# A third fixed expert in the second block of a two-layer mixture-of-experts transformer kernel

## The reference

```python
g_idx = jnp.argmax(g_logits, axis=-1)             # 1 of 4 groups a token
top_v, top_i = lax.top_k(e_sel, MOE_TOP_K)        # 2 of its 8 experts
eid = (g_idx[:, None] * MOE_EXPERTS_PER_GROUP + top_i).reshape(-1)
...
def expert_block(args):
    xb, e = args
    return (jax.nn.silu(xb @ w_gate[e]) * (xb @ w_up[e])) @ w_down[e]
```

## Time and profile before

| | |
|---|---|
| median of three runs | 1744.14 us |
| the profiled execution | 1743.2 us |
| its span | 1741.4 us |
| mean granted TensorE clock | 0.973 of full speed |
| TensorE busy | 1624.5 us (93%) |
| VectorE busy | 653.8 us (38%) |
| ScalarE busy | 373.2 us (21%) |

### The profile page before, as it was taken

One profiled execution on the slowest core, in us unless ns is written; L12 is line 12 of the kernel. 1 busy time (PEld: TensorE's weight loads), 2 busy tenths in 40 slices (PEclk: granted clock), 3 DMA queues, 4 the chain that ended last, 5 costly groups with the idle time before them and its releaser, 6 DMA issues.

```text
span 1741.4 us, 17712 instructions
## 1 busy us (share of the span) xinstructions
PE 1624.5 (93%) x6682; PEld 700.8 (40%) x6682; DVE 653.8 (38%) x1382; ACT 373.2 (21%) x919; POOL 71.2 (4%) x91
## 2 busy tenths in 40 slices
PE   5989998988999997998899999998889999979996
PEld 2435454462343332332344455444453333323332
DVE  2676665351323322323476122224531322322331
ACT  3023444231001010010410334333320101001000
POOL 1100000100000000000000000001000000000000
PEclk9999999999999998999999999998999999989999
DMA  9983823179999999999977021033389999999997
GB/s 353 372 308 100 288 97 146 52 285 389 430 426 426 425 428 427 427 428 419 364 240 243 1 97 49 1 124 123 141 365 420 427 423 427 429 426 426 428 427 293
DMA packets 109478, 526.64 MB, mean 302 GB/s; under 512 B 7921, under 2 KB 49122, under 8 KB 84682
## 3 DMA queue, kind: packets, MB, share of 16 engines
q1 hardware_dynamic: 80080, 486.56, 68.7%
q10 hardware_dynamic: 21322, 19.63, 3.6%
q0 software_dynamic: 7984, 19.22, 3.0%
HBM read 524.44 MB, written 8.48 MB: 306 GB/s over the span
## 4 chain that ended last, share of the span: by engine, by line
PE 81%; DMA 9%; DVE 5%; issue 2%; ACT 1%; SPq 1%; ACTq 0%; DVEq 0%
PE psum L2259 20%; PE psum L2290 11%; PE psum L2305 10%; PE psum L2016 10%; PE psum L1816 7%; PE psum L1988 4%; PE psum L1871 3%; DMA XN<-in_moe_w_up_dram 3%; DMA ring<-in_moe_w_up_dram 3%; DMA HT<-in_moe_w_down_dram 2%; PE psum L2237 2%; DVE W L1154 2%; DMA ring<-in_ada_w_dram 1%; PE psum L2123 1%; PE psum L1999 1%
## 5 line engine op out<-in xcount | busy, mean ns | idle before, releaser
L2259 PE MATMUL psum<-ring,V 128*32 128x512 f32 (+2 forms) x1376 | 352.3, 617 | 17.3 <-issue 9.4
L2305 PE MATMUL psum<-V,W 128*128 128x512 f32 x448 | 218.6, 613 | 3.6 <-DVE X L1606 1.1
L1606 DVE TENSOR_TENSOR X<-X,psum 128x512 f32<-128x512 f32 x224 | 153.7, 687 | 109.4 <-PE psum L2305 109.0
L2259 PEld LDWEIGHTS psum<-ring,V 128*32 128x32 f32 (+2 forms) x1376 | 115.9, 134 | 192.9 <-issue 192.6
L2290 PE MATMUL psum<-ring,V 128*64 128x512 f32 (+2 forms) x608 | 181.0, 596 | 0.8 <-issue 0.8
L1154 DVE SCALAR_TENSOR_TENSOR W<-ring,cact,W 128x512 f32<-128x512 f32 (+1 forms) x224 | 138.4, 618 | 7.7
L1046 ACT ACTIVATE V<-psum,modall,scls 128x128 f32<-128x128 f32 x216 | 81.2, 456 | 272.5 <-PE psum L2237 255.6
L2305 PEld LDWEIGHTS psum<-V,W 128*128 128x128 f32 x448 | 72.4, 188 | 148.5 <-DVE X L1606 85.3
L1055 ACT ACTIVATE V<-psum 128x512 f32<-128x512 f32 x28 | 16.7, 597 | 510.3 <-PE psum L2268 399.2
L2259 PE MATMUL psum<-HT,V 128*64 128x512 f32 (+2 forms) x224 | 102.4, 611 | 17.9 <-DMA XN<-in_moe_w_up_dram 17.5
L1816 PE MATMUL psum<-HT,ring 128*128 128x512 f32 x256 | 116.8, 602 | 0.0
(11 more groups left out here) (334 smaller groups left out, 1836.6 us busy)
## 6 DMA issues: line engine op xcount, KB each, us to landing
ring<-in_moe_w_up_dram SPq DMA_DIRECT2D x45, 2048.0 KB, 25.6
ring<-in_moe_w_gate_dram SPq DMA_DIRECT2D x41, 2048.0 KB, 25.3
ring<-in_moe_w_down_dram SPq DMA_DIRECT2D x38, 2048.0 KB, 25.4
ring<-in_ada_w_dram SPq DMA_DIRECT2D x16, 2048.0 KB, 15.8
HT<-in_moe_w_gate_dram SPq DMA_DIRECT2D x10, 2048.0 KB, 23.8
XN<-in_moe_w_up_dram SPq DMA_DIRECT2D x8, 2048.0 KB, 23.8
ring<-in_ada_w_dram ACTq DMA_DIRECT2D x16, 1024.0 KB, 5.2
T<-in_moe_w_up_dram SPq DMA_DIRECT2D x7, 2048.0 KB, 27.4
```

Source lines behind the costliest of these rows:

```text
L1606: return dve.tensor_tensor(x3[:, c, cols], x3[:, c, cols], sum_bank(p, hf, c), ALU.add)
L2259: ins = pe.matmul(bank[2 + 2 * i + b][half * w:(half + 1) * w, :], V[:, col:col + w], slot3(x)[:, k, :], start=(k == 0), stop=(k == KC - 1))
L2305: pe.matmul(sum_bank(p, hf, c), PICK[p % 2][:, c * P:(c + 1) * P], Y[:, hf * HALF:(hf + 1) * HALF], start=True, stop=True).then_inc(s["sum ...
```

## The change

Three things change. Expert 2 becomes the third fixed expert (`FIXED = 3`). The first four entries of `COLS` become 0, 5, 10, 1, so block 1 is now a pair and the four comes second; the pair holds expert 2 in its first half and the expert ranked highest below the wide ones in its other half (`rank_of`). Its matrices are loaded as gate, up, gate, up: loads 6 and 7 are expert 2's and need no ids, loads 8 and 9 are the ranked expert's. Block 2, the four, has loads 10 to 17, and block 1's downs are loads 18 and 19. The homes are dealt out anew (`HOMES`): in layer 0 T comes one place earlier, before ring buffer 4; in layer 1 T comes before ring buffer 5. And loads 9 and 10, the first into freed homes, are made in two halves: the first 1 MB of each when the gate pass of block 0 is half done (`first_gates`, a new semaphore), the second when that pass has ended. VectorE gets the arithmetic that puts expert 2 into its half block.

```diff
-HOMES = ((0, 1, 2, 4, 8, 7, 5, 3, 6), (1, 2, 3, 4, 0, 7, 5, 8, 6))
+HOMES = ((0, 1, 2, 8, 4, 7, 5, 3, 6), (1, 2, 3, 4, 0, 7, 8, 5, 6))
-FIXED = 2
+FIXED = 3
-COLS = [0, 10, 1, 5, 2, 11, 3, 6, 7, 12, 4, 8, 9, 13]
+COLS = [0, 5, 10, 1, 2, 11, 3, 6, 7, 12, 4, 8, 9, 13]
...
+    if COLS[p] == WIDE + 1 and half == 0:
+        return FIXED - 1
-    first = {1: FIXED + COLS[p] - 1, 2: FIXED + WIDE + 2 * (COLS[p] - WIDE - 1), 4: NARROW + 4 * (COLS[p] - WIDE - PAIRS)}
+    first = {1: FIXED + COLS[p] - 1, 2: FIXED + WIDE - 1 + 2 * (COLS[p] - WIDE - 1), 4: NARROW + 4 * (COLS[p] - WIDE - PAIRS)}
...
-    order = gate_up(0) + [(0, "d", half) for half in range(halves(0))] + gate_up(1)
+    order = gate_up(0) + [(0, "d", half) for half in range(halves(0))]
+    order += [(1, kind, half) for half in range(halves(1)) for kind in "gu"]
...
+REFILL = (len(HOMES[0]), len(HOMES[0]) + 1)
...
+                    if i in REFILL:
+                        sp.wait_ge(first_gates, l + 1)
+                        src = {"g": g, "u": u}[kind]
+                        sp.dma_start(slot(m + i)[:, 0:2 * D], src[:, 0:2 * D]).then_inc(w_in[SLOT[m + i]], 16)
+                        refill[i] = src
+                        if i == REFILL[1]:
+                            for x in REFILL:
+                                slot_free(m + x)
+                                sp.dma_start(slot(m + x)[:, 2 * D:4 * D], refill[x][:, 2 * D:4 * D]).then_inc(w_in[SLOT[m + x]], 16)
+                        continue
...
-                dve.tensor_tensor(extra, extra, wide_more, ALU.add)
+                dve.tensor_scalar(third, rank, -1.0, float(4 * WIDE), ALU.is_equal, ALU.mult)
+                step(dve.tensor_tensor(wide_more, wide_more, fixed_less, ALU.add))
                 step(dve.scalar_tensor_tensor(base, wide_base, 2.0, base, ALU.mult, ALU.add))
-                step(dve.tensor_tensor(extra, extra, fixed_less, ALU.add))
+                step(dve.scalar_tensor_tensor(base, wide_more, -1.0 / QP, base, ALU.mult, ALU.add))
+                step(dve.tensor_tensor(extra, extra, wide_more, ALU.add))
+                step(dve.tensor_tensor(base, base, third, ALU.add))
...
+                            if p == 0 and i == 0 and k == 3:
+                                ins.then_inc(first_gates, 1)
```

More of the change, by code:

```diff
@@ L156 @@
 AT = {b: n for n, b in enumerate(ORDER)}
-DMAS = [2 if kind == "kq" else 1 for kind, _, _ in ORDER]
+REFILL = (len(HOMES[0]), len(HOMES[0]) + 1)
+DMAS = [2 if kind == "kq" or kind == "moe" and i in REFILL else 1 for kind, _, i in ORDER]
 ARRIVED = [16 * sum(DMAS[i] for i in range(n + 1) if SLOT[i] == SLOT[n]) for n in range(len(ORDER))]
@@ L448, in program @@
         d_rest, odd_scale = [sem("d_rest0"), sem("d_rest1")], sem("odd_scale")
+        first_gates = sem("first_gates")
         half_sq, odd_ready = sem("half_sq"), sem("odd_ready")
@@ L530, in _ @@
                 m = AT["moe", l, 0]
-                expert, ranked = {}, False
+                expert, ranked, refill = {}, False, {}
                 for i, (p, kind, half) in enumerate(MOE_ORDER):
@@ L1414, in _ @@
                 wide_more, wide_base = (W[:, 784 + 32 * i:816 + 32 * i] for i in (3, 4))
+                third = W[:, 816:816 + E]
                 first_at, fixed_less = W[:, 3776:3784], W[:, 3784:3816]
@@ L1494, in _ @@
                 dve.tensor_copy(eid[:, :], bank[0][:, 0:E]).then_inc(s["eid_ready"].sem, 1)
-                step(dve.scalar_tensor_tensor(first_at.rearrange("p (c e) -> p c e", c=TC), M3[:, :, 0:FIXED], float(-P),
-                                              ranks[:, :, 0:FIXED], ALU.mult, ALU.add))
+                step(dve.scalar_tensor_tensor(first_at.rearrange("p (c e) -> p c e", c=TC), M3[:, :, 0:2], float(-P),
+                                              ranks[:, :, 0:2], ALU.mult, ALU.add))
                 dve.tensor_tensor(FIRST.rearrange("p (a n) -> p a n", n=2 * QP),
```

## The result

The changed kernel takes 1750.91 us (median of 16 runs, 1746.96 to 1753.8) against 1744.37 us for the kernel before (16 runs, 1743.36 to 1748.19). The ratio is 1.0033, with a 95% interval of 1.0026 to 1.0040: slower by about 6 us. I had forecast 1745.0 with a range of 1739.0 to 1750.0, and held a change too small to tell (under about 0.2%) for the likeliest case.

The account below looks back on a forecast made before the run. The weight stream of 96 matrices per layer was taken to set the end. Layer 0's +1.5 and layer 1's -0.6 made +0.9 us: 1743.2 to 1744.1 profiled, 1745.0 as median, range 1739.0 to 1750.0.

Parts of the forecast that it names:

- The 1.6 us are gone: Layer 0, load 15: the 1.6 us gained before the ids is lost, since it lands at 440.1 again.
- routing costs nothing: VectorE's routing: three more steps, about 0.7 us, fit in the 2.2 us of cover by TensorE's row products.
- Rival (c): Refill halves: each of four added DMAs holds the queue 2.6 us, together +5.5 us, 1749.6; chance 0.05.
- Rival (b): Block 1's gate pass, both layers: 1.2 GHz all through, 14.2 us, costing 9.8 us, 1753.9; chance 0.13.
- In a full queue a load has no fixed part: Load stream: 1 MB loads land 2.4 us apart, half of 4.9, so splitting adds no queue time.
- Layer 0, +1.5: Layer 0's net: load 16 waits for block 1's up pass and lands later; +2.0 by the nearest row, +1.5 taken.
- 0.9 us to spare: Layer 0, load 19: could land at 461.6 at the earliest, the stream brings it at 462.5, so no further gap.
- landing 1344.9, against 1345.7 before. That is 0.8 us earlier; I take 0.6: Layer 1, load 19: homes come at 1337.4, so it lands 0.8 us earlier; the layer's term is -0.6 us.
- My bounds: Block 1's gate pass at 7.1 to 14.2 us: load 16 from 1.8 earlier to 5.3 later; layer 1, 2.0 to 4.5.
- The signs of the moves ahead of the ids: Loads moved before the ids: 1.6 us ahead in layer 0, then lost; 2.0 us ahead in layer 1, -0.6 kept.

Follow-up runs that it names:

- e7: The changed kernel with loads 6 and 7 (expert 2's gate and up) held until the ids are there: 1750.43 us, kernel before 1744.91.
- e1: The changed kernel with loads 9 and 10 made whole again instead of in halves: 1750.49 us, kernel before 1745.19.
- e2: The changed kernel with the homes of loads 16 and 17 exchanged, and so on every nine loads: 1747.21 us, kernel before 1745.19.
- e5: The changed kernel once more, unedited, for a second profile: 1751.95 us, kernel before 1744.91.
- e4: The changed kernel with TensorE's branch on the overflow flag moved behind block 4: 1740.35 us, kernel before 1745.19.
- e3: The kernel before with TensorE's branch on the overflow flag moved behind block 4, nothing else: 1744.00 us, unedited 1745.19.
- e9: The kernel before without TensorE's branch on the overflow flag and the loop behind it: 1744.51 us, unedited 1745.63.
- e10: The changed kernel without TensorE's branch on the overflow flag and the loop behind it: 1743.59 us, kernel before 1745.63.

## Why the prediction was wrong

**What held.** The profile's bound was read rightly: the stream sets the end, and the place that decides is the branch and the passes behind it. T at 318, a dry queue before load 8 (3.3 us forecast, about 4 by the DMA share between 384 and 394), load 15 issued at the end of the gate pass and load 16 about 7 us later, a branch of 6 us: all came as written. "The 1.6 us are gone" agrees with e7, where what is loaded early measures nothing, and that routing costs nothing is shown by the issue of load 8 in layer 0 (389.98 against 390.09; three steps of 0.2 us make 0.6, not 0.7, which changes nothing). Rival (c), a fixed cost of the halves, gave the nearest number, 1749.6, and is refuted by e1: a right size from a wrong cause. Rival (b) had the right place and the wrong size: the two passes took 16.1 and 16.3 us, not 21.3. "In a full queue a load has no fixed part" held too: in e2, layer 0, the halves 9, 10, 9, 10 landed at 403.2, 405.5, 408.0 and 410.4, 2.3 to 2.5 us apart. (The Trainium skill's section that the prediction names beside it, DMA: Bandwidth & Descriptors, Anatomy of one DMA, gives its 2.0 us for DMAs that GpSimd issues; these loads are SP's.)

**Layer 0, +1.5.** The sum was right (+1.6), but by luck: its steps were not. The gate pass of the pair was shorter than the four's (9.3 us, not 11.1), the up pass ended at 437.6 instead of 439.5, and load 16 landed at 445.02, where it had landed before. The loss came at the step that I had given "0.9 us to spare": load 19. It left at 452.7, 1.4 earlier than forecast, and its successors were late all the same (load 21 at 471.9, 1.1 behind before).

**The step that failed** is the one on load 19 and layer 1: "landing 1344.9, against 1345.7 before. That is 0.8 us earlier; I take 0.6". Two things were wrong in it.

First, I treated a release that comes just in time as free: the later of issue + 7.5 and predecessor + 4.9. In the eight cases load 19 left 0.4 to 4.2 us before its predecessor landed, and came 0.7 us later than that on average, up to 1.7 (e1, layer 0); after, by the loads behind it, 1.1 us in layer 0 and 1.5 in layer 1 (load 20 at 1353.8, less 4.9, against 1339.9 + 7.5), and the window there shows 353 GB/s, not 427. That is all of the 0.8 that layer 1 was to be earlier and of the 0.9 to spare in layer 0.

Second, I read the release times of layer 1 from one execution and gave them no spread. They vary with the execution: row products 8.8 to 10.4 us and passes 15.7 or 16.3 us with TensorE's clock (0.83 and 0.70, 0.90 and 0.85), the branch 5.9 to 6.7 us, for which no run shows a reason. In the profile after all three were near their long end: load 19 left at 1339.9, 2.5 us behind the 1337.4 of the forecast; in e5 at 1337.0. My bounds moved only the one gate pass, and I let the stream's own order take the rest. But with homes late at loads 15, 16 and 19 there is no queue left to take it, and in that profile the delay went to the end. The two together, 2.5 of late issue and 1.5 of landing, less the 0.8 that I had in hand, are the 3.2 us by which load 20 was late. Of layer 1's 5.2 us, 1.5 are there at the issue of load 8 (31.4 against 29.9 us from load 4), 3.2 at the landing of load 20, and the last 2.0 build up behind it. That last part is mostly not the change: this stretch was 366.4 us in the profile before and between 366.9 and 368.4 in all others, so the profile that I summed from was itself a lucky one there.

**The signs of the moves ahead of the ids** were then misjudged as a whole. I held them at zero behind the late homes in layer 0, rightly, and did not ask what the pair at the second place costs in return: between the end of block 0 and the gate pass of block 2 the four had given back eight homes in two passes, the pair gives back four in the same two passes, which take as long (7.1 us each at full clock), and the eight come a block later. e2 frees load 16 of this and gains half; e4 lets the gate pass start 5.4 us and end 7.6 us earlier, and the loss becomes a gain.

**What stays open.** How much of the 6.5 us the late homes account for. The four profiles with the old branch and loads 16 and 17 not swapped give +6.8 (after), +5.4 (e1), +2.5 (e5) and +2.3 (e7) by stages, 4 us on average, while the medians are 5.3 to 7.0 above the kernel before. In e5 and e7 layer 1 lost nothing up to load 20 (105.2 and 105.1 us from load 4's issue to load 20's landing, 105.1 before, 108.3 after). The profiled execution of e7 is at its kernel's median (1750.64), and of its 7.4 us over the span before 5.1 lie outside the two stretches. Outside them the profiles scatter between 2.9 us less and 5.1 us more than before, and no run tells whether that belongs to the change. That the changed kernel scatters more is not shown either: 6.8 us over 16 runs against 4.8 over 16, but other comparisons have 10.5 over 12 for it and 7.8 over 30 and 9.3 over 35 for the kernel before.

In the profiles, e2 stands only about 0.5 us below e5 by stages, and in medians 4.7 us (3.7 below the first 16 runs). Both profiled executions are among the fastest of their kernels, 1744.58 and 1746.41; where the longer ones lose their time was not seen. And no run puts the pair second without expert 2's early loads and the new homes, so what the order of the blocks costs by itself is argued from these runs, not measured.

## What to carry to other kernels

A gain at the front of a transfer stream is kept only if no buffer behind it is released late: list, for each refill, the pass that frees its buffer, and put stalls of TensorE (a branch, here) where the queue is deepest. That blocks which free many buffers per us of TensorE should come first is what these runs suggest, not what one of them tested. Where no cushion is left in front of a late buffer, sum from both ends of the spread of the durations ahead of it and not from one execution. And test a neutral-looking part together with the obstacle removed: the halves, and expert 2's early loads, each measured zero alone and 2 to 3 us once the branch had moved.

## What the runs showed of the hardware

- A compare and branch on TensorE to a far target stood for 5.9 to 7.7 us in all twelve profiles that have it, and behind block 4, with the queue full, it showed in no stage time (e3 +0.5 against e9 +0.9, e4 -5.0 against e10 -4.0). The Trainium skill (Runtime: NRT & Kernel Launch, Instruction fetch mechanics) says that a taken branch out of the prefetched pages stalls until its target is fetched. The traces agree in kind: in the branch of the profile before, from 414.9 to 421.3, the instruction queue moved one packet of 16 KB, at 418.8. The page gives no time.
- The copy of the rows to DRAM (2 MB, on GpSimd's queue) took 13.5 us before and 24.5 us after in layer 1, where SP now had four loads in the queue beside it, and 22.1 and 24.4 us in layer 0; with loads 6 and 7 held (e7) it took 13.6 and, in layer 0, 15.0. It cost nothing, since XN waited for TensorE (load 8 left 0.2 us behind the row products), but it is far from an even share: loads of 2 MB landed every 6 to 8 us meanwhile.
- In a full queue a load of 1 MB took 2.3 to 2.5 us of the stream and one of 2 MB 4.9 us, so splitting a load cost no time there (e2, layer 0).
